# A hybrid decoder step on one core: the samples' outer products in fp32r on 32 rows, and four convolution tiles and one channel set beside the last head

## What is computed

```python
proj = einsum('btd,de->bte', rmsnorm(x), w_in)        # 7168 columns: 3 x 1024 for the convolution, 4 x 1024 for retention
u = cg * hc;  y_conv = bg * sum(full[:, j:j+t] * conv_w[j] for j in range(3))   # full: state_conv, then u
# retention, 8 heads of 128; rotary on q and k; for the 8 samples a chunk is one token:
s_new = g * s + k^T v            # one 128 x 128 outer product per sample and head
o = q @ s_new
y_ret = silu(g) * groupnorm(o)
out = concat(y_conv, y_ret) @ w_out
```

## Time and profile before

| | |
|---|---|
| median of 3 executions | 2183.91 us (2183.71 to 2185.83) |
| the profiled execution | 2185.02 us |
| its span in the profile | 2183.4 us |
| TensorE busy | 2144.7 us, 98% |
| VectorE busy | 1422.3 us, 65% |
| ScalarE busy | 924.1 us, 42% |
| mean granted clock of TensorE | 0.989 |

### The profile page before, as it was taken

The page is one execution under the profiler, slowest core; times in us unless marked ns, Lnnn a source line. Parts: engine busy times, 40 slices in busy tenths (PEclk is TensorE's granted clock), DMA queues, the critical chain, the costliest instruction groups (busy, mean ns, idle before and its releaser), DMA issues.

```text
span 2183.4 us, 46575 instructions
## 1 busy us (share of the span) xinstructions
PE 2144.7 (98%) x18559; PEld 2113.5 (97%) x18559; DVE 1422.3 (65%) x2660; ACT 924.1 (42%) x1255; POOL 60.3 (3%) x78
## 2 busy tenths in 40 slices
PE   7999999998999999999999999999999999999997
PEld 7999799997999999999999999999999999999997
DVE  7666666557788957765657565666655556666665
ACT  5544433332344434444444443434444344444444
POOL 1000000000000000000000000000000000000000
PEclk9999899998999999999999999999999999999999
DMA  7555355553455556676556565656566555666653
GB/s 270 166 178 171 128 174 184 203 177 112 154 167 182 183 177 192 209 227 222 191 197 203 194 206 189 214 190 210 198 199 203 183 202 199 211 213 203 204 176 126
DMA packets 114050, 414.09 MB, mean 190 GB/s; under 512 B 13248, under 2 KB 13504, under 8 KB 113632
## 3 DMA queue, kind: packets, MB, share of 16 engines
q1 hardware_dynamic: 101088, 365.29, 51.2%
q0 software_dynamic: 8480, 30.24, 4.3%
q10 hardware_dynamic: 4320, 16.22, 1.9%
HBM read 387.36 MB, written 24.26 MB: 189 GB/s over the span
## 4 chain that ended last, share of the span: by engine, by line
PE 87%; DVE 1%; ACT 0%; issue 0%; DVEq 0%; ACTq 0%
PE bank L837 28%; PE bank L838 28%; PE bank L839 27%; PE bank L997 2%; PE bank L960 1%; DVE pair L1108 0%; DVE xlo L1115 0%; DVE acc L1700 0%; PE bank L895 0%; PE bank L906 0%; DVE xhi L1113 0%; PE bank L866 0%; PE bank L1023 0%; DVE s_new L1191 0%; PE bank L912 0%
## 5 line engine op out<-in xcount | busy, mean ns | idle before, releaser
L837 PE MATMUL bank<-xhi,whi 128*128 128x264 f32 x4096 | 1177.8, 288 | 18.1 <-DVE wlo L1075 10.0
L1075 DVE TENSOR_TENSOR wlo<-raw,whi 128x1024 fp32r<-128x1024 f32 x688 | 829.7, 1223 | 540.0 <-ACT whi L585 537.6
L838 PE MATMUL bank<-xlo,whi 128*128 128x264 f32 x4096 | 1165.6, 285 | 0.0
L839 PE MATMUL bank<-xhi,wlo 128*128 128x264 f32 x4096 | 1165.5, 285 | 0.0
L585 ACT CAST whi<-raw 128x1024 fp32r<-128x1024 f32 x688 | 708.6, 1047 | 651.4 <-PE bank L839 645.0
L837 PEld LDWEIGHTS bank<-xhi,whi 128*128 128x128 f32 x4096 | 775.9, 189 | 30.4 <-DVE wlo L1075 15.2
L838 PEld LDWEIGHTS bank<-xlo,whi 128*128 128x128 f32 x4096 | 776.3, 190 | 0.3
L839 PEld LDWEIGHTS bank<-xhi,wlo 128*128 128x128 f32 x4096 | 772.4, 189 | 0.0
L837 PE MATMUL bank<-wexp_hi,whi 128*128 128x264 f32 x1152 | 328.4, 285 | 0.0
L838 PE MATMUL bank<-wexp_lo,whi 128*128 128x264 f32 x1152 | 327.0, 284 | 0.0
L839 PE MATMUL bank<-wexp_hi,wlo 128*128 128x264 f32 x1152 | 326.7, 284 | 0.0
(11 more groups left out here) (203 smaller groups left out, 1088.7 us busy)
## 6 DMA issues: line engine op xcount, KB each, us to landing
raw<-halves SPq DMA_DIRECT2D x688, 512.0 KB, 3.5
hid<-gates ACTq DMA_DIRECT2D x30, 528.0 KB, 4.6
gates<-stage POOLq DMA_DIRECT2D x17, 768.0 KB, 7.3
s_old<-ret_state POOLq DMA_DIRECT2D x8, 512.0 KB, 5.9
ret_sample<-s_new POOLq DMA_DIRECT2D x8, 512.0 KB, 3.9
gates<-route_mem POOLq DMA_DIRECT2D x5, 768.0 KB, 7.3
acc<-xT SPq DMA_DIRECT2D x4, 528.0 KB, 6.2
yT<-acc SPq DMA_DIRECT2D x8, 264.0 KB, 2.4
```

What stands on the lines that cost most here:

```text
L837: nc.tensor.matmul(out, whi[:, s, c], mh[c], start=start and c == 0, stop=False)
L838: nc.tensor.matmul(out, whi[:, s, c], ml[c], start=False, stop=False)
L839: mm = nc.tensor.matmul(out, wlo[:, s, c], mh[c], start=False, stop=stop and c == HALF - 1)
L1075: v.tensor_tensor(wlo[:, s], raw[:, s], whi[:, s].bitcast(F32), ALU.subtract).then_inc(lo_done, 1)
```

## The change

1. Each sample's v and k are split on VectorE into a high and a low part (new function parts_of: a copy to fp32r and a subtraction, 16 columns each), and four combinations are stacked: v_parts holds high, low, high, low and k_parts high, high, low, low, 8 columns each. The small transposes take these 32 columns as they take 8 before, vs_tok, ks_tok and v_diag have 32 rows, the table "diag" is repeated four times, and ks_tok and v_diag are fp32r. The contraction over 32 rows then gives all four partial products. turn waits for two new semaphores.
2. head(8) has tiles again: convolution tiles 0 to 3 stand between its pieces of attention, with ahead(0) to ahead(3) on ScalarE and VectorE.
3. Channel 0 of the convolution stands on VectorE behind head(8), ahead of the last mean_square, the low halves of tile 5 and normed(7). So the y parts 7 and 8 change their order (y_turn). Channels 1 to 7 follow; their low halves of weights are made at the same places as before, but for those already made.
4. The loops over the convolution are unrolled on all engines.

```diff
+STACK = 4 * NSAMPLE
     put("diag", np.eye(P)[:, :NSAMPLE])
+    at, n = CONSTS["diag"]
+    c[0:STACK, at:at + n] = np.tile(np.eye(NSAMPLE), (STACK // NSAMPLE, 1))
...
+        v_parts = sb("v_parts", [P, 2, 2, NSAMPLE], F32R, mix)
+        k_parts = sb("k_parts", [P, 2, 2, NSAMPLE], F32R, mix)
+        vs_tok = sb("vs_tok", [STACK, P], F32, mix)
+        ks_tok = sb("ks_tok", [STACK, P], F32R, mix)
+        v_diag = sb("v_diag", [STACK, NSAMPLE, P], F32R, mix)
...
+        def y_turn(c):
+
+            return {HEADS - 1: HEADS, HEADS: HEADS - 1}.get(c, c)
+
+        def loads_tiles(h):
+
+            return not isinstance(h, int) or h <= HEADS
...
             load_root(1)
             r0 = W_CONV // 2
-            with act.Fori(0, HEADS // 4) as i:
-                for j in range(4):
-                    for n in range(3):
-                        k = 3 * j + n
-                        ahead(r0 + i * 6, k)
+            for k in range(BANKS, T_CONV):
+                ahead(r0, k)
...
+                pe.wait_ge(v_parts_ready, p + 1)
+                nc.tensor.transpose(bank[4][0:STACK, 2 * P:3 * P], stacked(v_parts), ident)
                 for t in range(2):
                     nc.tensor.transpose(bank[5][:, t * P:(t + 1) * P], kT[:, t * P:(t + 1) * P], ident)
-                nc.tensor.transpose(bank[5][0:NSAMPLE, 2 * P:3 * P], kT[:, NPROMPT:T], ident)
+                pe.wait_ge(k_parts_ready, p + 1)
+                nc.tensor.transpose(bank[5][0:STACK, 2 * P:3 * P], stacked(k_parts), ident)
...
+                    elif loads_tiles(h):
+                        tile(W_CONV // 2, k, W_CONV // BANKS, k, xhi, xlo)
...
+            for k in range(BANKS, T_CONV):
+                tile(W_CONV // 2, k, W_CONV // BANKS, k, xhi, xlo)
...
+            def parts_of(x, hi, lo, ready):
+
+                twice = x[:, NPROMPT:T].unsqueeze(1).to_broadcast([P, 2, NSAMPLE])
+                ch.did(v.tensor_copy(hi, twice))
+                ch.wait()
+                v.tensor_tensor(lo, twice, hi.bitcast(F32), ALU.subtract).then_inc(ready, 1)
+
+            def values_out(h):
+                tile_done(h * 2, 0)
                 v.tensor_tensor(vT[:], bank[0][:, 0:T], rx[:], ALU.mult).then_inc(bank_free[0], 1)
+                dve.wait_ge(bank_free[0], h + 1)
+                parts_of(vT, v_parts[:, :, 0], v_parts[:, :, 1], v_parts_ready)
...
                     rotate(kT, 1, "cosk", "sink", h * 2)
-                    if not first:
-                        ahead(r, 3)
+                    dve.wait_ge(rot_ready, h * 2 + 1)
+                    parts_of(kT, k_parts[:, 0], k_parts[:, 1], k_parts_ready)
+                if loads_tiles(h) and not first:
+                    ahead(r, 3)
...
+            def conv_ahead(k):
+
+                if k > BANKS:
+                    ahead(W_CONV // 2, k)
...
+            head(HEADS)
             ch.did(v.memset(up[:, 0:2], 0.0))
...
+            channel(0)
+            mean_square(1.0 / HD, GN_EPS, bank[7][:, 0:T], [(var_done, HEADS)])
+            ahead(W_CONV // 2, BANKS)
+            normed(HEADS - 1)
+            for c in range(1, HEADS):
+                channel(c)
```

More of the change, by code:

```diff
@@ L79 @@
 assert C_TAIL + (GROUPS - MIXED) * GROUP == TILES
+assert W_CONV == BANKS * HEADS and W_CONV % (2 * BANKS) == 0
 FREED_U0 = (T_HEADS + T_CONV) // BANKS
@@ L388, in build @@
         rot_ready = sem("rot_ready")
+        v_parts_ready = sem("v_parts_ready")
+        k_parts_ready = sem("k_parts_ready")
         turned = sem("turned")
@@ L651, in head @@
                     first_squares()
-                elif tiles:
+                elif loads_tiles(h):
                     ahead(r, 0)
@@ L656, in head @@
                     nc.scalar.copy(v_tok[:], bank[4][:, 0:2 * P].rearrange("p (c e) -> p c e", c=2))
-                    nc.scalar.copy(vs_tok[:], bank[4][0:NSAMPLE, 2 * P:3 * P]).then_inc(tok_ready, 1)
+                    nc.scalar.copy(vs_tok[:], bank[4][0:STACK, 2 * P:3 * P]).then_inc(tok_ready, 1)
                 if norm:
                     root(h)
-                if tiles and not first:
+                if loads_tiles(h) and not first:
                     ahead(r, 1)
@@ L669, in head @@
                     swap(1)
-                    if not first:
-                        ahead(r, 2)
+                if loads_tiles(h) and not first:
+                    ahead(r, 2)
                 if att:
@@ L871, in norm_waits, with stacked @@
                              for s in range(2))
+            def stacked(parts):
+                return parts[:].rearrange("p a b s -> p (a b s)").bitcast(F32)
             def turn(p):
@@ L934, in _ @@
             head(HEADS)
-            with pe.Fori(0, HEADS // 4) as i:
-                for k in range(12):
-                    tile(W_CONV // 2 + i * 6, k, W_CONV // BANKS + i * 3, k, xhi, xlo)
+            for k in range(BANKS, T_CONV):
+                tile(W_CONV // 2, k, W_CONV // BANKS, k, xhi, xlo)
             def out_tiles(i):
@@ L944, in out_tiles @@
                     if first and k == 0:
-                        w = tuple({c: [(y_ready, s * HALF + c + 1)] for c in range(HALF)} for s in range(2))
+                        w = tuple({c: [(y_ready, y_turn(s * HALF + c) + 1)] for c in range(HALF)} for s in range(2))
                     if not first:
@@ L1172, in attention_in @@
                                 of_head("zeta", p), None, ALU.mult)
-                v.tensor_copy(ks_tok[:], bank[5][0:NSAMPLE, 2 * P:3 * P])
+                v.tensor_copy(ks_tok[:], bank[5][0:STACK, 2 * P:3 * P])
                 v.tensor_tensor(scored[:], bank[6][:, 0:2 * P].rearrange("p (c e) -> p c e", c=2),
@@ L1177, in attention_in @@
                 dve.wait_ge(tok_ready, p + 1)
-                v.tensor_tensor(v_diag[:], vs_tok[:].unsqueeze(1).to_broadcast([NSAMPLE, NSAMPLE, P]),
-                                table("diag")[0:NSAMPLE].unsqueeze(2).to_broadcast([NSAMPLE, NSAMPLE, P]),
+                v.tensor_tensor(v_diag[:], vs_tok[:].unsqueeze(1).to_broadcast([STACK, NSAMPLE, P]),
+                                table("diag")[0:STACK].unsqueeze(2).to_broadcast([STACK, NSAMPLE, P]),
                                 ALU.mult).then_inc(att_ready, 1)
@@ L1206, in normed @@
                 if not (isinstance(p, int) and p == 0):
-                    dve.wait_ge(y_ready, p)
+                    dve.wait_ge(y_ready, y_turn(p) if isinstance(p, int) else p)
                 ch.did(v.tensor_tensor(yv[:], dev[:], rstd, ALU.mult))
@@ L1227, in head @@
                 tiles, att, norm = steps_of(h)
-                if tiles:
+                if loads_tiles(h):
                     ahead(r, 0)
@@ L1231, in head @@
                     first_norm()
-                    values_out(r)
+                    values_out(h)
                 if norm:
@@ L1273, in _ @@
                 head(h)
-            with ch.fori(2, HEADS, 10) as h:
+            with ch.fori(2, HEADS, 12) as h:
                 head(h)
-            for h in range(HEADS, HEADS + 2):
-                head(h)
-            ch.did(v.memset(up[:, 0:2], 0.0))
[L1281 to L1318, removed]
@@ new lines, in conv_ahead, with channel @@
+            def conv_ahead(k):
+                if k > BANKS:
+                    ahead(W_CONV // 2, k)
+            def channel(c):
+                r, o4, j = W_CONV // 2, W_CONV // BANKS, c
+                sel = bass.ds(c, 1)
+                conv_ahead(3 * j)
+                dve.wait_ge(y_ready, y_turn(HEADS + c))
+                ch.did(v.tensor_copy(us[:, 0:2, :], sconv[:, sel].rearrange("p c a b -> p (c a) b")))
+                conv_ahead(3 * j + 1)
+                bh, bc, bb = ((3 * j + n) % BANKS for n in range(3))
+                tile_done(r, 3 * j)
+                v.tensor_tensor(hcs[:], bank[bh][:, 0:T], rx2[:], ALU.mult).then_inc(bank_free[bh], 1)
+                tile_done(r, 3 * j + 1)
+                dve.wait_ge(bank_free[bh], o4 + (3 * j) // BANKS + 1)
+                ch.did(v.tensor_tensor(us[:, 2, :], bank[bc][:, NPROMPT:T], hcs[:, NPROMPT:T], ALU.mult))
+                v.tensor_tensor(up[:, 2:], bank[bc][:, 0:NPROMPT], hcs[:, 0:NPROMPT], ALU.mult)\
+                    .then_inc(bank_free[bc], 1)
+                dve.wait_ge(bank_free[bc], o4 + (3 * j + 1) // BANKS + 1)
+                ch.wait()
+                taps = [cw[:, sel, n:n + 1].rearrange("p c n -> p (c n)") for n in range(3)]
+                v.tensor_copy(conv_out[:, sel, 0:2].rearrange("p c n -> p (c n)"), up[:, NPROMPT:])
+                ch.did(v.tensor_copy(conv_out[:, sel, 2:].rearrange("p c n -> p (c n)"),
+                                     us[:, 1:3, :].rearrange("p a b -> p (a b)")))
+                v.tensor_scalar(yv[:, 0:NPROMPT], up[:, 0:NPROMPT], taps[0], None, ALU.mult)
+                ch.did(v.tensor_scalar(yv[:, NPROMPT:], us[:, 0, :], taps[0], None, ALU.mult))
+                for n in range(1, 3):
+                    ch.wait()
```

(11 more changed lines are left out.)

7 lines of the change are left out of this document (1 added, 6 removed).

## The result

The kernel before took 2183.8 us and the changed one 2165.5 us (medians of four and of three executions; a fourth of the changed kernel took 11173 us and is left out). The ratio is 0.9914, with a 95% interval of 0.9895 to 0.9934: faster by 0.9%, 18.3 us. The forecast was 2163.0 with a range of 2159.5 to 2167.5. The profiled execution took 2165.5 us with a span of 2163.9, so 19.5 less than the span of before.

The account below looks back on a forecast made before the run. TensorE, busy 98% of the span, was taken to bound the kernel. Terms -10.1 - 13.6 + 0.5 + 2.2 = -21.0 us took the profiled 2185.0 to 2164.0, and the median, 1.1 lower, to 2163; range 2159.5 to 2167.5.

Parts of the forecast that it names:

- The outer products: Heads 1 to 7: two fp32r instructions replace four, 1.44 us gained per head, 10.1 us in all.
- The four new operations on VectorE: Splits of v and k: covered by spare VectorE time in heads 1 to 7; 0.5 us lost in head 0.
- The last head: From its first variance matmul to the first output tile: 145.4 us instead of 159.04, 13.6 us gained.
- The wait at tile 6: Convolution: tile 6's low halves of weights come late on VectorE, 2.2 us lost, between 0 and 3.5.
- rival D: VectorE doesn't catch up after normed(7); all seven remaining channels begin with a wait and clock fall: 2187 us, chance 0.02.
- rival B: The wait at tile 6 also makes the clock fall, costing 1.5 us: 2164.5, up to 2166.5 us; chance 0.25.
- Unrolling: The convolution's loops unrolled: costs instruction fetch alone, counted at nothing.
- A: No wait at tile 6, the walk of VectorE's order being 2 us too long: 2160.7 us, chance 0.17.
- C: The fp32r outer products give little, a head gaining 0.96 us or less: 2167 to 2174 us, chance 0.05.
- the last one: Tiles beside the last head still wait for its attention, so the change doesn't do what it says; chance in 0.01.

Follow-up runs that it names:

- experiment 6: The changed kernel with each head's two outer-product matmuls done twice into the same banks; span 2168.1 us, period 29.79 us.
- experiment 7: The changed kernel with ks_tok and v_diag on 128 rows, rows 32 to 127 zeroed once by GpSimd; median 2162.6 us, ratio 0.9898 to the kernel before.
- experiment 8: The changed kernel with the split of v behind that of k in the first head; span 2164.2 us, wait for qT 0.43 us.
- experiment 3: The changed kernel with tile 6's two low halves of weights made before channel 1; median 2163.9 us, ratio 0.9907 to the kernel before.
- experiment 2: The changed kernel with fp32 outer products on 8 rows, without the split; span 2174.7 us, ratio 0.9961 to the kernel before.
- experiment 9: The kernel with tiles beside the last head and fp32 outer products, on 128 rows instead of 8; span 2170.6 us, ratio 0.9939 to the kernel before.
- experiment 4: The changed kernel with one unused addition of 1024 columns on VectorE between normed(7) and channel 1; span 2166.4 us, wait at tile 6 2.73 us.
- experiment 5: The changed kernel with two unused additions of 1024 columns on VectorE between normed(7) and channel 1; span 2168.4 us, wait at tile 6 3.99 us.

## Why the prediction was right

The direction, the size and the place of each term came out as forecast; the forecast of the span missed by 1.5 us of 21, nearly all in one term.

- **The outer products**: 1.44 us a head forecast, 1.25 measured. The step that failed is the price of the pair, 0.47 us by columns of the tile's matmul. One matmul does cost 235 ns (experiment 6). What I left out is the border from 128-row operands to 32-row ones and back, over which TensorE did not load weights ahead (experiment 7). I had taken the next neighbour's row and not asked what stood on either side of it. Seven heads: 1.3 us of the 1.5. The border was in the price of before too, so not all of the 1.91 us was matmul. The figure that the Trainium skill (TensorE: Matmul & The Clock Gate, section "Wait — 56ns, not 53.3ns?") gives, 215.7 ns for 512 columns, was further from the trace's 235 than the 234 by columns, as 112.5 against 120.8 ns had hinted.
- **The four new operations on VectorE**: hidden in heads 1 to 7 (TensorE has no wait there), in the first head 0.42 us of wait and 0.1 of a later start against 0.5. Right, and experiment 8 shows the cause.
- **The last head**: 13.6 gained less 2.2 for the wait, so 11.4; measured 11.6. It is 29.07 us long where I had 29.12. That fits by chance: the pair is 0.19 us longer than forecast, and here the variance doesn't wait for ScalarE's squares, which come early since there are no rotations (deviation at 268.34, the variance at 272.11).
- **The wait at tile 6**: the walk through VectorE's order, in us after 243.04, against the trace: hcs 26.0, measured 25.7 to 26.2; bank product 29.0, measured 28.8; mean_square 30.5, measured 30.5; low halves of tile 5 done 34.8, measured 34.8; tile 6's first low half begins 42.1, measured 41.6; TensorE ready 41.0, measured 41.3. So a wait of 1.73 and not 2.2. The two small misses both shorten it. Channels 2 to 7 have no wait in the changed kernel, so rival D (VectorE without time for the channels) is out, and experiment 3 removes the one wait by order alone.
- **The clock behind that wait** (rival B): it didn't fall, neither here nor in experiments 2 and 6 to 9, whose profiles all have a wait of 1.72 or 1.73 us at tile 6. Experiments 4 and 5 show that the rival was a near one: at 2.73 us of wait it falls and costs 1.5 us more. The forecast's own 2.2 us would have been in between, and no run says what that would do; that there was no fall may be owed to the wait coming out shorter, which is luck. The rule of the Trainium skill (TensorE: Matmul & The Clock Gate, section "What's actually happening") is that throttled is the default and activity releases it. The trace agrees where the clock fell, in experiments 4 and 5.
- **Unrolling** the convolution's loops, counted at nothing, shows no cost: the last 20 tiles take 5.82 us each, with the wait at tile 6 taken off.
- **What follows**: 0.3 us given back behind the first output tile, for which I had nothing. 1.3 for the pairs and 0.3 here, less 0.2 in the last head, make the difference between the spans of 2162.4 and 2163.9. The other 1.0 us between forecast and median is the profiled execution of before, 1.1 above its median, which I carried over to the changed kernel, whose profiled execution was at its median.
- Rivals A, C and the last one are out by the same rows: there was a wait, the form gives what its columns say, and no tile waited for the last head's attention.

## What to carry to other kernels

When a stage leaves the main engine idle, look for work of the next stage that depends on nothing in it, and count what was lost there in clock too: here TensorE was idle for 4.5 us, and the tiles beside the last head alone (experiment 2) took 10.3 us off the way to the first output tile. Then walk the helper engine's order through the new stage, step by step with durations from rows; that walk found the next wait within half a us, and moving two conversions ahead of it took it away. And price an operation together with its neighbours: operands with another number of rows between full ones cost 0.3 us here, which zeroed rows gave back.

## What was not expected of the hardware

- Going from operands of 128 rows to 8 or 32 and back cost 0.34 us a head in fp32r and 0.37 in fp32 (periods 29.30 to 28.96, and 30.56 to 30.19), and neither the pair's weights nor the next tile's were loaded ahead.
- The clock fell once with TensorE busy without a gap. It was 0.6 us behind 1.9 us of fp32 matmuls on 8 rows (experiment 2, one profile), and in the same place with the same matmuls on 128 rows it didn't. The kernel before has the 8-row pair in the same place and kept its clock, so the rows alone don't explain it; what does isn't shown. Busy time alone doesn't tell whether the clock will hold.
- A fall of the clock came 2.2, 2.8 and 4.9 us after TensorE had stopped (the kernel before, experiments 4 and 5), once when it had already been at work again for 0.9 us. The row of the wait alone doesn't show it; the rows behind it have to be read too.
